# Second attention's scores as three bfloat16 products, with queries and keys of each pair split by GpSimd

## What is computed

```python
q = q.reshape(Bsz, S, ATT_HEADS, ATT_HEAD_DIM) * (ATT_HEAD_DIM ** -0.5)
k = k.reshape(Bsz, S, ATT_HEADS, ATT_HEAD_DIM)
...
scores = jnp.einsum('bnqrhe,bnkrhe->bnrhqk', qb, kk).astype(jnp.float32)
```

## Time and profile before

| | us |
|---|---|
| time, median of 3 runs (1832.68 to 1833.72) | 1833.22 |
| the profiled execution's own time | 1831.29 |
| its span | 1829.4 |
| second attention (item 0 of pair 0 to the last `weigh`) | 1304 to 1751 |
| TensorE busy | 1775.0 |
| VectorE busy | 1168.8 |
| ScalarE busy | 762.1 |
| GpSimd busy | 739.9 |

### The profile page before, as it was taken

The page is one execution under the profiler, slowest core; times in us unless marked ns, Lnnn a source line. Parts: engine busy times, 40 slices in busy tenths (PEclk is TensorE's granted clock), DMA queues, the critical chain, the costliest instruction groups (busy, mean ns, idle before and its releaser), DMA issues.

```text
span 1829.4 us, 27353 instructions
## 1 busy us (share of the span) xinstructions
PE 1775.0 (97%) x10441; PEld 919.2 (50%) x10606; DVE 1168.8 (64%) x2282; ACT 762.1 (42%) x1432; POOL 739.9 (40%) x696
## 2 busy tenths in 40 slices
PE   8999999999999999999999999999999999999998
PEld 5534445454444556444444555554455555555543
DVE  5668799999997777222545677764255455544547
ACT  4533652444213667213322559442234444444510
POOL 0520463462831315669413300316525633562460
PEclk9999999999999999999999999999999999999999
DMA  9011011222411102231311221112111111111422
GB/s 398 14 58 43 39 47 64 93 81 94 177 47 58 43 34 99 116 138 47 149 47 71 81 92 70 58 59 98 60 35 49 53 56 33 31 49 55 152 112 92
DMA packets 41601, 145.87 MB, mean 80 GB/s; under 512 B 6432, under 2 KB 12832, under 8 KB 37248
## 3 DMA queue, kind: packets, MB, share of 16 engines
q1 hardware_dynamic: 37248, 120.56, 18.1%
q0 software_dynamic: 4224, 23.56, 3.3%
HBM read 117.82 MB, written 23.13 MB: 77 GB/s over the span
## 4 chain that ended last, share of the span: by engine, by line
PE 78%; DVE 13%; ACT 3%; DMA 3%; issue 2%; POOL 1%; SPq 0%; DVEq 0%; ACTq 0%; POOLq 0%
PE ps L1267 39%; PE ps L1738 14%; PE ps L1261 4%; DVE small L2479 3%; DVE arena L2231 2%; PE ps L1377 2%; PE ps L1383 2%; PE ps L1317 2%; PE ps L1400 2%; PE ps L1757 2%; PE ps L1343 2%; PE ps L1304 2%; DMA hT<-in_mods 1%; PE ps L1544 1%; PE ps L1697 1%
## 5 line engine op out<-in xcount | busy, mean ns | idle before, releaser
L1267 PE MATMUL ps<-hT,W 128*128 128x512 bf16 x2196 | 491.5, 379 | 12.2 <-ACT arena L1841 4.2
L1267 PEld LDWEIGHTS ps<-hT,W 128*128 128x128 bf16 x2256 | 217.6, 98 | 274.4 <-issue 11.7
L917 POOL TENSOR_TENSOR W<-W 128x512 bf16<-128x512 f32 x118 | 135.5, 1184 | 268.6 <-DMA W<-in_loads 200.9
L1267 PE MATMUL ps<-W,arena 128*128 128x512 bf16 x916 | 206.9, 380 | 1.2
L1913 ACT ACTIVATE arena<-arena,small 128x128 f32<-128x128 f32 (+9 forms) x192 | 123.1, 642 | 157.5 <-DVE small L2308 129.2
L1920 ACT ACTIVATE arena<-arena,small 128x128 f32<-128x128 f32 (+9 forms) x192 | 114.0, 640 | 126.4 <-DVE small L2320 105.7
L1267 PEld LDWEIGHTS ps<-W,arena 128*128 128x128 bf16 x936 | 91.2, 97 | 112.0
L2479 DVE TENSOR_SCALAR_CACHE_REDUCE small<-arena,small 128x640 bf16<-128x640 f32 (+1 forms) x124 | 126.5, 1077 | 1.1
L1267 PE MATMUL ps<-arena,W 128*128 128x512 bf16 x569 | 124.5, 379 | 1.1 <-POOL arena L978 0.7
L2945 DVE TENSOR_TENSOR arena<-ps,arena 128x512 f32<-128x512 f32 x70 | 51.0, 728 | 104.1 <-PE ps L1738 104.1
L1738 PE MATMUL ps<-arena,W 128*128 128x512 bf16 x461 | 107.9, 379 | 1.6
(11 more groups left out here) (383 smaller groups left out, 3179.5 us busy)
## 6 DMA issues: line engine op xcount, KB each, us to landing
W<-in_loads SPq DMA_DIRECT2D x20, 2048.0 KB, 8.4
W<-in_groups SPq DMA_DIRECT2D x51, 256.0 KB, 3.9
W<-in_loads SPq DMA_DIRECT2D x5, 1792.0 KB, 7.1
gates_scratch<-arena SPq DMA_DIRECT2D x32, 256.0 KB, 2.0
arena<-gates_scratch POOLq DMA_DIRECT2D x2, 4096.0 KB, 13.7
arena<-sums_scratch SPq DMA_DIRECT2D x16, 512.0 KB, 3.8
W<-in_mods SPq DMA_DIRECT2D x2, 2048.0 KB, 17.2
hT<-in_mods SPq DMA_DIRECT2D x2, 2048.0 KB, 21.5
```

Source lines behind the costliest of these rows:

```text
L917: last = nc.gpsimd.tensor_tensor(low(v), v, high(v), ALU.subtract)
L1267: last = mm(o, left[:, :, a], moving, start=(k == 0 and (a, b) == PRODUCTS[0]), stop=(k == steps - 1 and (a, b) == PRODUCTS[-1]))
```

## The change

1. After a q/k group is added up, GpSimd splits it. `split_queries` writes the low part of 512 queries in place (one subtraction). `split_keys` copies the high part of 512 keys to one plane of `pair_k[j % 2]` and writes the low part to the other (a copy and a subtraction). The float32 keys now land elsewhere first (`key_rows`: the other `pair_k` for pair 0, `z_tanh` for the others). Two of each for a pair.
2. For pair 0 GpSimd does it ahead of `make_group(0)`, for pair j + 1 at the end of loop step j, behind the two `make_group` (for j = 6 behind the split of woA0).
3. `scores` makes each product as three bfloat16 ones, queries as weights from `parts`, keys moving from `planes`: near 6 matmuls for 4, far 24 for 16. It waits for `s_qparts` and `s_kparts` in place of the reads.
4. Two waits for the shared area: ScalarE's gate tanh (line 2207) for the split keys, VectorE's 3rd read for the gate made.

```diff
@@ -473,6 +473,7 @@
         res_stage = [area(29696 + 512 * q, 512) for q in range(4)]
         base, corner = area(29696, 512), area(30208, 512)
         z_tanh = area(30720, 1024)
+        key_rows = [pair_k[1]] + [z_tanh] * 7
         lng = area(24576, 1024)
         lnb = area(25600, 1024)
 
@@ -549,6 +550,8 @@
         s_gated2 = sem("pair_gate_made")
         s_resback = sem("state_rows_back")
         s_far = [sem(f"far_values_placed{x}") for x in range(2)]
+        s_kparts = sem("pair_keys_split")
+        s_qparts = sem("pair_queries_split")
         s_tsum = sem("token_sums_made")
         s_thigh = sem("token_sums_high")
         s_tlow = sem("token_sums_low")
@@ -1096,6 +1099,23 @@
                 for name, _, _, _ in BLOCK_PRODUCTS:
                     nc.gpsimd.tensor_tensor(low(v[name]), v[name], high(v[name]), ALU.subtract).then_inc(s_block, 1)
 
+
+            def split_queries(j, half):
+
+                v = pair_q[j % 2][:, 512 * half:512 * half + 512]
+                nc.gpsimd.tensor_tensor(low(v), v, high(v), ALU.subtract).then_inc(s_qparts, 1)
+
+            def split_keys(j, half):
+
+                span = slice(512 * half, 512 * half + 512)
+                v, made = key_rows[j][:, span], planes(pair_k[j % 2])
+                nc.gpsimd.tensor_copy(made[:, span, HIGH], high(v))
+                nc.gpsimd.tensor_tensor(made[:, span, LOW], v, high(v), ALU.subtract).then_inc(s_kparts, 1)
+
+            pool.wait_ge(s_free, FIRST["pair0"] + 4)
+            for half in range(2):
+                split_queries(0, half)
+                split_keys(0, half)
             make_group(0)
             make_group(1)
 
@@ -1126,6 +1146,18 @@
                     split("woA1")
                 for g in range(2 * j + 2, min(2 * j + 4, GROUPS)):
                     make_group(g)
+                if j < 7:
+                    g = 2 * j + 1
+                    pool.wait_ge(s_first, BASE_READS * (g + 1))
+                    split_queries(j + 1, 0)
+                    pool.wait_ge(s_read, SUM_READS * g + FAR_CORNER)
+                    split_keys(j + 1, 1)
+                    pool.wait_ge(s_read, SUM_READS * g + SECOND_FIRST)
+                    split_keys(j + 1, 0)
+                    pool.wait_ge(s_read, SUM_READS * g + FIRST_SECOND)
+                    split_queries(j + 1, 1)
+                    pool.wait_ge(s_kparts, 2 * j + 4)
+                    pool.wait_ge(s_qparts, 2 * j + 4)
             pair_done(7)
             pool.wait_ge(s_att[1]["weighted"], 32)
             nc.gpsimd.dma_start(lng, rows[2]).then_inc(s_row, 16)
@@ -1362,27 +1394,29 @@
                 def scores(n):
 
                     j, i = items[n][3], items[n][2]
-                    if i == 0 and j:
-                        pe.wait_ge(s_first, 2 * BASE_READS * j)
-                        pe.wait_ge(s_read, SUM_READS * (2 * j - 1) + SECOND_FIRST)
-                    elif i == 0:
-                        pe.wait_ge(s_free, FIRST["pair0"] + 4)
-                    elif i == 4 and j:
-                        pe.wait_ge(s_read, 2 * SUM_READS * j)
+                    if i == 0:
+                        pe.wait_ge(s_qparts, 2 * j + 1)
+                        pe.wait_ge(s_kparts, 2 * j + 2)
+                    elif i == 4:
+                        pe.wait_ge(s_qparts, 2 * j + 2)
                     if n >= 1:
                         pe.wait_ge(sems["biased"], 2 * n)
-                    q, k = pair_q[j % 2], pair_k[j % 2]
+                    q, k = parts(pair_q[j % 2]), planes(pair_k[j % 2])
                     far = far_keys(i)
-                    for x in range(2):
-                        last = mm(ps[:, 2 + x, far:window(i)], q[halves[x], i * P:(i + 1) * P],
-                                  k[halves[x], max(i - 1, 0) * P:(i + 1) * P], start=True, stop=True)
+                    for a, b in PRODUCTS:
+                        for x in range(2):
+                            last = mm(ps[:, 2 + x, far:window(i)], q[halves[x], i * P:(i + 1) * P, a],
+                                      k[halves[x], max(i - 1, 0) * P:(i + 1) * P, b],
+                                      start=((a, b) == PRODUCTS[0]), stop=((a, b) == PRODUCTS[-1]))
                     if far:
-                        for r in range(RES):
-                            for x in range(2):
-                                at_ = i * P + RUN * r
-                                last = mm(ps[RUN * r:RUN * r + RUN, 2 + x, 0:far],
-                                          q[halves[x], at_:at_ + RUN], of_residue(k[halves[x]], r, 0, far),
-                                          start=True, stop=True)
+                        for a, b in PRODUCTS:
+                            for r in range(RES):
+                                for x in range(2):
+                                    at_ = i * P + RUN * r
+                                    last = mm(ps[RUN * r:RUN * r + RUN, 2 + x, 0:far],
+                                              q[halves[x], at_:at_ + RUN, a], of_residue(k[halves[x], :, b], r, 0, far),
+                                              start=((a, b) == PRODUCTS[0]), stop=((a, b) == PRODUCTS[-1]),
+                                              skip_group_check=True)
                     last.then_inc(sems["scores"], 1)
 
                 def turn(m):
@@ -1878,7 +1912,7 @@
                         last = A(pair_q[j % 2][:, span].rearrange("p (t r s) -> p t r s", t=4, r=RES),
                                  bank.rearrange("p (t s r) -> p t r s", t=4, r=RES), ACT.Copy)
                     elif what == "k":
-                        last = A(pair_k[j % 2][:, span], bank, ACT.Copy)
+                        last = A(key_rows[j][:, span], bank, ACT.Copy)
                     else:
                         last = A(pair_vT[j % 2][:, span], bank, ACT.Copy)
                 elif name[:3] == "woS":
@@ -2199,6 +2233,7 @@
                 if j < 8 and place == 1 and i == 4:
                     act.wait_ge(s_read, SUM_READS * (2 * j - 1))
                     act.wait_ge(s_first, BASE_READS * (2 * j - 1))
+                    act.wait_ge(s_kparts, 2 * j)
                     if j >= 2:
                         act.wait_ge(s_gated2, j - 1)
                     else:
@@ -2922,7 +2957,7 @@
                     return
                 dve.wait_ge(s_prod, PER_GROUP * g + q + 1)
                 first = mixA[:, j, :] if i < 4 else pair_q[j % 2]
-                second = pair_vT[j % 2] if i < 4 else pair_k[j % 2]
+                second = pair_vT[j % 2] if i < 4 else key_rows[j]
                 add, bank = base, ps[:, BLOCK_PRODUCTS[q][2], :]
                 if q == 1:
                     dve.wait_ge(s_first, BASE_READS * g + 1)
@@ -2935,6 +2970,8 @@
                 elif q == 4:
                     dve.wait_ge(s_read, SUM_READS * g + CORNER_MADE)
                     to, add = second[:, 512:1024], corner
+                    if i >= 4:
+                        dve.wait_ge(s_gated2, j)
                 elif q == 5:
                     to = second[:, 0:512]
                 elif i < 4:
```

## The result

The changed kernel takes 1812.51 us (median of 4, 1811.75 to 1815.74) against 1833.34 us (median of 4 as well): ratio 0.9892, 95% interval 0.9878 to 0.9905. The forecast was 1811, range 1805 to 1823.

A forecast was written before the change was run, and what follows sets the result against it. TensorE was taken to bound the kernel; near 1.2 plus far 1.8 less 0.2 for extra sets, over seven pairs and 2.2 in pair 7, gave 22.4 us off 1831.3: 1808.9, median 1811, range 1805 to 1823.

The forecast's parts named there:

- What bounds the kernel: Second attention: TensorE is busy nearly throughout pairs 0 to 6, so time taken from its instructions comes off pair by pair.
- Near scores: Near products in three passes for four, constant 0.15 us: 0.47 us for 256 columns, 0.31 for 128, 1.2 us less a pair.
- The lower bound of 0.6 us a pair: Smallest near-score gain: the constant stays at 0.21 us and each pass pays some 15 ns more.
- Far scores: Far products: element distance sets the twofold rate; keys 8 bytes apart run at full rate, 0.31 to 0.43 us, 1.8 less a pair.
- Rival 1: Far scores: eight tiles at once keep the twofold rate, 0.7 us less a pair, in all 1820 us; chance 0.28.
- Extra sets: Scores: three near and three far sets for two and two, 12 ns each beyond columns, costing 0.2 us a pair.
- The sum: Whole kernel: 2.8 to 2.9 us a pair, seven pairs 20, pair 7 2.2; 22.4 off 1831.3 gives 1808.9, median 1811.
- GpSimd: Splits of 5.7 us a pair stay hidden, with 4 us left in pairs 1 to 6 and 2 in pair 7.
- Rival 4: GpSimd's splits at the slow pace, 3.08 us for 1.11, cause 20 us of waits: 1831 to 1834; chance 0.04.
- It would cost what it is late, once: GpSimd's splits at pair 7's first scores: if the cover were gone, the cost is the lateness, once; counted at nothing.
- Rivals 2 and 3: Scores: small matmuls' starts bind, 1825 us, chance 0.10; second and third sets' loads can't be hidden, 1840, chance 0.05.
- The two pages: Trainium skill rules: starts about 25 ns apart, whole change giving 5 us; two hits per 16-byte SBUF line give full rate.

## Why the prediction was right, and where it was not

- **What bounds the kernel: right.** TensorE's time came off one for one, pair by pair (2.41 us of 2.46 that the two kinds save alone).
- **Near scores: the mechanism right, the constant mis-sized.** Forecast 0.47 and 0.31 us, measured 0.43 and 0.28. 0.43 is three passes of 107 ns and 0.11 us. The constant went down to the lower bound given, "what the mode change alone would be". If that is what it is, the bfloat16 load doesn't show at all, but no run separates the two. The term was 1.2 us a pair and measured 1.54. The lower bound of 0.6 us a pair doesn't follow from its own words: with the constant at 0.21 and 15 ns more for each of three passes, 0.4 are left.
- **Far scores: the step that failed.** The rows left two causes for the twofold rate, and I took the distance of the elements, rightly: both runs with dense keys and the one with spread near keys show it. But I then let 8 bytes count as near enough for full rate, and that is wrong: four elements apart is slow in bfloat16 as in float32. The term was 1.8 us a pair and measured 0.92. Rival 1 had the size (0.7, and 0.74 us at 224 columns) with a cause that the runs refute. The rows of before had float32 at 4 bytes (full rate) and at 16 (half), and no bfloat16 operand at a distance, so what 8 bytes would do was open and deserved a rival of its own; it had none.
- **Extra sets: nothing.** 0.2 us a pair was counted for them. With 0.11 + 3 x 0.107 for the near scores there is no room for it.
- **The sum.** 1.54 + 0.92 for 1.2 + 1.8 - 0.2: 2.41 in place of 2.8 to 2.9. Pair 7 gave 2.45, all of what a full pair gives, where I counted 2.2: its waits moved with it. Forecast of the profiled execution 1808.9, measured 1812.4. That the median came nearer, 1811 against 1812.5, is luck: errors of opposite sign met in the terms (0.5 us a pair too little for near and extra sets, 0.9 too much for far), and the last step, 1.9 us up from the profiled execution to the median, had no counterpart after: there the profiled one, 1812.38, is at the median. With the later pair of medians the gain is 17.4 us, so it is 17 to 21 us by the runs and 19 by the traces; 1.6 us of that spread is the stretch at a lower granted clock in the second trace of the changed kernel.
- **GpSimd: right.** The splits cost nothing (1.0003). They end 4.7 and 3.2 us ahead, for 4 and 2 forecast, and the doubled ones are late by 1.1 us in pair 7 alone, as the gap says. Rival 4's slow pace never came. "It would cost what it is late, once" is an upper bound for 1.1 us, which cost 0.7, and too low for the trebled splits: 33 us for 24 late, since TensorE ran slow for a while behind most of the waits.
- **Rivals 2 and 3: refuted.** Starts don't bind (24 matmuls of 64 columns on neighbouring keys in 0.21 us, 9 ns each), and loads stay hidden there under sets of 27 ns.
- **The two pages.** The Trainium skill, "TensorE: Matmul & The Clock Gate", section "Wait — 56ns, not 53.3ns?", has starts 25 ns apart at the least. Applied to eight tiles side by side, as the prediction did, that doesn't hold: they start 9 ns apart. The Trainium skill, "SBUF — State Buffer", section "Door 1: The DMA port swizzle (why `[64,N]` ≈ `[32,N]`)", would have bfloat16 at distance four at full rate, as two hits fall in one line. It takes twice the time, while float32 at the same 8 bytes does not. The same note of the Trainium skill lists four float32 among the distances that are free, which the prediction passed over. They are not: 0.93 us for 0.54 at 224 columns. The measurements decide against the note for these matmuls.

## What to carry to other kernels

Before splitting float32 products into three, look at the operand's distance: four elements apart cost the moving side a factor of two in either type, and for the far products neighbours gave more than the split (1.47 us of a pair in float32, for 0.92). For both kinds of scores the split gave 2.41 us a pair, the split and the layout together 3.24. A cover for a helper engine is read as the gap between its last piece and the consumer's start; here it told the wait for doubled splits (1.1 us, for 0.7 to 1.2 expected) and fell short for trebled ones in pair 7 (5.7 for 4.5 to 5). When two terms of a sum rest on unknown rates, a right total says little about either; look for each in the trace.

## What was not expected of the hardware

- A moving operand at distance two runs at nearly full rate (0.45 us for 0.43), at distance four at half (0.78), in bfloat16; in float32 224 columns take 0.54 us dense and 0.93 at distance four. It goes by elements, not bytes: 8 bytes are slow in bfloat16 and fast in float32. What happens at three, or beyond four, was not tried.
- Eight tiles on dense columns take one column a cycle each, all at once: 1.25 ns for three passes.
- A wait of 3.25 us on TensorE cost another 1.75 us after it (12 matmuls in 4.45 us for 2.70), with a granted clock of 0.74 in the 6.5 us behind it; one of 3.38 us in the next pair, and those of 2.18 and 1.06 us, were followed by full clock. In all, 24 us of waits made 33.
- At the slow level, 1.2 GHz of 2.4, TensorE's starts lie twice as far apart: behind the wait of 5.67 us, at a granted clock of 0.51 (1724.5 to 1727), groups of transposes start 0.42 us after each other, and 0.22 at full clock.
